# A chunked recurrence in 64x64 products: half of the heads keep their token rows in the other half of the partitions

## The reference

```python
def step(state, inp):
    r_t, w_t, k_t, v_t, a_t, b_t = inp
    sa = jnp.einsum('bhij,bhj->bhi', state, a_t)
    state = state * w_t[:, :, None, :] + sa[..., None] * b_t[:, :, None, :] + v_t[..., None] * k_t[:, :, None, :]
    return state, jnp.einsum('bhij,bhj->bhi', state, r_t)
...
mean = jnp.mean(y, axis=-1, keepdims=True)
var = jnp.mean(jnp.square(y - mean), axis=-1, keepdims=True)
yn = ((y - mean) * lax.rsqrt(var + GN_EPS)).reshape(B, S, RWKV_DIM) * gn_w + gn_b
bonus = (jnp.sum(r * k * r_k, axis=-1, keepdims=True) * v).reshape(B, S, RWKV_DIM)
return (yn + bonus) * g
```

## Time and profile before

| | before |
|---|---|
| median of 3 runs | 3677.74 us |
| profiled execution | 3676.37 us, span 3674.2 us |
| TensorE busy | 3536.7 us, 96% |
| VectorE busy | 1827.8 us, 50% |
| ScalarE busy | 1145.6 us, 31% |
| GpSimd busy | 490.6 us, 13% |

### The profile page before, as it was taken

One profiled execution on the slowest core, in us unless ns is written; L12 is line 12 of the kernel. 1 busy time (PEld: TensorE's weight loads), 2 busy tenths in 40 slices (PEclk: granted clock), 3 DMA queues, 4 the chain that ended last, 5 costly groups with the idle time before them and its releaser, 6 DMA issues. The chain is left out here.

```text
span 3674.2 us, 52665 instructions
## 1 busy us (share of the span) xinstructions
PE 3536.7 (96%) x21944; PEld 2888.8 (79%) x21944; DVE 1827.8 (50%) x2090; ACT 1145.6 (31%) x1325; POOL 490.6 (13%) x445
## 2 busy tenths in 40 slices
PE   7999999899999999999999999999999998999998
PEld 5578888778888888887578887887778996768886
DVE  7655244335244563346655244564786554455242
ACT  3632123222122232222632134233662222232222
POOL 1111011011011011010111013000241111111011
PEclk9999999889999999999999999999999998999998
DMA  3132323212322323223133323343321113313231
GB/s 124 60 96 92 102 93 97 69 58 94 101 92 92 103 92 103 92 95 107 60 96 95 100 92 104 103 132 95 95 73 60 38 44 130 103 46 103 92 103 58
DMA packets 313946, 329.07 MB, mean 90 GB/s; under 512 B 22819, under 2 KB 305446, under 8 KB 313255
## 3 DMA queue, kind: packets, MB, share of 16 engines
q1 hardware_dynamic: 306999, 302.87, 25.9%
q0 software_dynamic: 4464, 19.40, 1.6%
q10 hardware_dynamic: 2304, 4.20, 0.3%
HBM read 311.76 MB, written 14.68 MB: 89 GB/s over the span
## 5 line engine op out<-in xcount | busy, mean ns | idle before, releaser
L476 PE MATMUL ps<-xh,wh 128*128 128x512 f32 x2424 | 959.4, 396 | 24.4 <-DVE wl L417 21.0
L476 PE MATMUL ps<-xl,wh 128*128 128x512 f32 x2424 | 946.2, 390 | 0.0
L476 PE MATMUL ps<-xh,wl 128*128 128x512 f32 x2424 | 946.2, 390 | 0.0
L417 DVE TENSOR_TENSOR wl<-raw,wh 128x2048 fp32r<-128x2048 f32 (+2 forms) x287 | 642.6, 2240 | 457.4 <-ACT wh L412 456.8
L412 ACT ACTIVATE wh<-raw 128x2048 fp32r<-128x2048 f32 (+2 forms) x287 | 527.1, 1837 | 712.3 <-PE ps L476 678.2
L476 PEld LDWEIGHTS ps<-xh,wh 128*128 128x128 f32 x2424 | 457.0, 189 | 134.8 <-issue 36.2
L476 PEld LDWEIGHTS ps<-xl,wh 128*128 128x128 f32 x2424 | 457.2, 189 | 99.3 <-issue 5.8
L476 PEld LDWEIGHTS ps<-xh,wl 128*128 128x128 f32 x2424 | 456.8, 188 | 96.0
L476 PE MATMUL ps<-hh,wh 128*128 128x512 f32 x1280 | 498.3, 389 | 1.2 <-DVE wl L417 0.9
L476 PE MATMUL ps<-hl,wh 128*128 128x512 f32 x1280 | 497.9, 389 | 0.0
L476 PE MATMUL ps<-hh,wl 128*128 128x512 f32 x1280 | 497.9, 389 | 0.0
(11 more groups left out here) (403 smaller groups left out, 3660.4 us busy)
## 6 DMA issues: line engine op xcount, KB each, us to landing
raw<-in_mlp_w SPq DMA_DIRECT2D x128, 1024.0 KB, 5.2
raw<-in_ffn_w SPq DMA_DIRECT2D x32, 1024.0 KB, 5.3
raw<-in_w_in SPq DMA_DIRECT2D x31, 1024.0 KB, 5.3
raw<-in_a_w_in SPq DMA_DIRECT2D x20, 1024.0 KB, 5.0
raw<-in_c_w_in SPq DMA_DIRECT2D x12, 1024.0 KB, 5.1
raw<-in_a_w_out SPq DMA_DIRECT2D x16, 640.0 KB, 4.1
raw<-in_b_w_in SPq DMA_DIRECT2D x8, 1024.0 KB, 5.3
raw<-in_xa_wkv SPq DMA_DIRECT2D x8, 1024.0 KB, 5.6
```

The costliest lines, as they stand in the source:

```text
L417: nc.vector.tensor_tensor(wl[:, p.slot(su), 0:n], raw[:, p.slot(su), 0:n], wh[:, p.slot(su), 0:n], ALU.subtract).then_inc(lower, 1)
L476: last = nc.tensor.matmul(banks[mt][:, 0:st.n], wt[at_, slot, k, mt * P:mt * P + P], ops[oi][at_, kk, 0:st.n], start=k == 0 and su == 0 an ...
```

## The change

Heads of group 1 (q 4-7) keep everything that is indexed by token (TM, X, V, B and K turned, U, TLB, TLK) in the other half of the partitions: `toks(h, q)` is half h for q below 4 and the other half above, `chan(h, q)` is always h. Their products then have operands on one half and output on the other, or as before where both are channels or both tokens. `together` issues products in turn: for each i, both halves of the first list, then both halves of the second, which may be group 1 beside group 0, or two different steps.

The transposed inverse Z is summed in PSUM: `first_z` starts a bank of each group, `more_z` of each level accumulates onto it, and ScalarE copies the sum out after each level; VectorE's additions to Z go. X starts from a copy of a product too (`first_x`). The products and transposes of the next chunk move into the levels of this one as fillers; V and B are turned into one pair of banks and copied together. Where group 1 accumulates a product over operands on one half onto one over the other half, TensorE waits for itself (`ck_crossed`). The state's additions are done by VectorE after the X copies of the next chunk. The head norm's sums and spread alternate between both halves, and the scaling is done in two halves. Many semaphores elsewhere share a name now, with the counts adjusted; nothing else changes there.

```diff
+    def chan(h, q):
+        return HP[h]
+    def toks(h, q):
+        return HP[h] if q < 4 else HP[1 - h]
+    def together(*fns):
+        for i in range(4):
+            last = [[fn(h, i) for h in range(2)][-1] for fn in fns]
         return last
...
+            first_x = lambda h, q: mm(ps[YX[q // 4]][toks(h, q), cols(q)], TI[toks(h, q), q], i64[toks(h, q), :], start=True, stop=True)
+            first_z = lambda h, q: mm(ps[ZB[q // 4]][chan(h, q), cols(q)], i64[toks(h, q), :], TI[toks(h, q), q], start=q % 4 == 0, stop=True, skip_group_check=True)
+            more_x = lambda h, q: mm(ps[YX[q // 4]][toks(h, q), cols(q)], Z[chan(h, q), q], Yt[chan(h, q), q], start=True, stop=True)
+            more_z = lambda h, q: mm(ps[ZB[q // 4]][chan(h, q), cols(q)], Yt[chan(h, q), q], Z[chan(h, q), q],
+                                     start=False, stop=True, skip_group_check=True)
...
             for l in range(1, 6):
-                for g in range(2):
-                    pe.wait_ge(s(f"ck_x{g}"), 5 * c + l)
-                    heads_of(g, lambda h, q: mm(ps[YB[g]][h, cols(q)], TM[l % 2][h, q], X[h, q], start=True, stop=True)).then_inc(s(f"ck_y{g}"), 1)
...
+                times = lambda h, q: mm(ps[YX[q // 4]][chan(h, q), cols(q)], TM[l % 2][toks(h, q), q], X[toks(h, q), q],
+                                        start=True, stop=True)
+                pe.wait_ge(s("ck_x0"), 5 * c + l)
+                pe.wait_ge(s("ck_tm"), 6 * c + l + 1)
+                together(group(0, times))[0].then_inc(s("ck_y0"), 1)
+                if l > 1:
+                    pe.wait_ge(s("ck_y_copied1"), 5 * c + l - 1)
+                    pe.wait_ge(s("ck_z1"), 6 * c + l - 1)
+                    last = together(group(1, more_x), group(1, more_z))
...
+                if l == 4 and more:
+                    pe_products(pe, c + 1, 0, "ck_bprod")
...
+                pe.wait_ge(s("ck_y_copied0"), 5 * c + l)
+                pe.wait_ge(s("ck_z0"), 6 * c + l)
+                if l < 5:
+                    together(group(0, more_x))[0].then_inc(s("ck_xm0"), 1)
+                pe.wait_ge(s("ck_x1"), 5 * c + l)
+                last = together(group(0, more_z), group(1, times))
...
+            together(group(0, ds_b), group(1, ds_b))
+            together(group(0, ds_k), group(1, ds_k))[1].then_inc(s("ck_ds"), 1)
+            together(group(0, o_u), group(1, o_u))[1].then_inc(s("ck_crossed"), 1)
+            together(group(0, o_state))
+            pe.wait_ge(s("ck_crossed"), 2 * c + 2)
+            together(group(1, o_state))[0].then_inc(s("ck_yout"), 1)
...
+    def act_z(act, c, g, l):
+        act.wait_ge(s(f"ck_zm{g}"), 6 * c + l + 1)
+        act.activation(half(Z, g), half(b3(ZB[g]), g), ACT.Copy).then_inc(s(f"ck_z{g}"), 1)
```

More of the change, by code:

```diff
@@ L1602, in build @@
+        pool.wait_ge(s("pool_tables"), 4)
     mm = nc.tensor.matmul
     PB = (0, 1)
[L1605 to L1613, removed]
-        tok = slice(c * CH, c * CH + CH)
[L1616 to L1628, removed]
+    YX, ZB = (4, 5), (6, 2)
+    WB = (7, 3)
+    def chan(h, q):
[5 more added lines that the diff above has]
+            last = [[fn(h, i) for h in range(2)][-1] for fn in fns]
+        return last
@@ new lines, in group, with pe_turn, turn @@
+    def group(g, fn):
+        return lambda h, i: fn(h, 4 * g + i)
+    def pe_turn(pe, c, which, banks):
+        tok = slice(c * CH, c * CH + CH)
+        srcs_ = ((lambda h, q: VT[chan(h, q), q, tok], c64, 0), (lambda h, q: BT[chan(h, q), c, q], i64, 1)) if which == 0 \
+            else ((lambda h, q: KT[chan(h, q), c, q], i64, 0),)
+        def turn(src, eye, at_):
+            return lambda h, q: mm(ps[banks[q // 4]][toks(h, q), at_ * 256 + q % 4 * CH:at_ * 256 + q % 4 * CH + CH],
+                                   src(h, q), eye[chan(h, q), :], start=True, stop=True)
+        for e in srcs_:
+            last = together(group(0, turn(*e)), group(1, turn(*e)))
+        last[-1].then_inc(s("ck_turned"), 1)
@@ L1630, in HB, with pe_products, product, SB @@
+    def pe_products(pe, c, which, done):
+        def product(h, q):
+            k = chan(h, q)
+            return mm(ps[PB[q // 4]][toks(h, q), q % 4 * P:q % 4 * P + P], (BT, KT)[which][k, c, q],
+                      AR[k, c, q].rearrange("p a n -> p (a n)"), start=True, stop=True)
+        together(group(0, product), group(1, product))[-1].then_inc(s(done), 1)
+    RT = small[:, 4:12]
     def HB(c):
-        return 3 if c < NC - 1 else 4
+        return 0 if c < NC - 1 else 6
+    def SB(c):
+        return (0, 1) if c < NC - 1 else (4, 5)
@@ L1633, in pe_head_sums @@
     def pe_head_sums(pe, c):
         pe.wait_ge(s("hd_squared"), c + 1)
[L1636 to L1637 removed]
+        for i in range(4):
+            for g in range(2):
+                last = mm(ps[HB(c)][HP[g], 2 * i:2 * i + 2], hs[c][:, 4 * g + i], headones[:, 0:P:64], start=True, stop=True)
         last.then_inc(s("hd_sums"), 1)
@@ L1642, in pe_head_spread @@
         pe.wait_ge(s("hd_inverse"), c + 1)
[L1643 to L1646, removed]
+        for i in range(4):
+            for g in range(2):
+                for e in range(2):
+                    last = mm(ps[SB(c)[g]][HP[e], cols(4 * g + i)], RT[HP[g], 2 * i + e:2 * i + e + 1].to_broadcast([64, CH]),
+                              i64[HP[g], :], start=True, stop=True)
         last.then_inc(s("hd_spread"), 1)
@@ L1686, in pe_chunks @@
                     if c:
+                        if more:
+                            pe.wait_ge(s("ck_turned_copied"), 4 * c + 6)
+                        pe_head_sums(pe, c - 1)
                         pe.wait_ge(s("ck_state"), c)
[L1688 to L1695, removed]
@@ L1736, in pe_chunks @@
-            last.then_inc(s("ck_yout"), 1)
-            if c < NC - 1:
-                pe_turns(pe, c + 1)
+                    pe.wait_ge(s("ck_kmasked"), c + 1)
+                    together(group(0, w0_tok), group(1, w0_tok))[1].then_inc(s("ck_crossed"), 1)
+                if l == 3:
+                    together(group(0, w0_state))[0].then_inc(s("ck_w0"), 1)
+                    pe.wait_ge(s("ck_crossed"), 2 * c + 1)
+                    together(group(1, w0_state))[0].then_inc(s("ck_w0"), 1)
+                    if c:
+                        pe_head_spread(pe, c - 1)
@@ new lines, in pe_chunks @@
+            pe.wait_ge(s("ck_z0"), 6 * c + 6)
+            together(group(0, u_of))[0].then_inc(s("ck_u"), 1)
+            if more:
+                pe.wait_ge(s("ck_bmasked"), c + 2)
+                pe_products(pe, c + 1, 1, "ck_kprod")
+            pe.wait_ge(s("ck_z1"), 6 * c + 6)
+            together(group(1, u_of))[0].then_inc(s("ck_u"), 1)
+            last = together(group(0, o_v), group(1, o_v))
+            if more:
+                pe.wait_ge(s("ck_turned_copied"), 4 * c + 8)
+            pe.wait_ge(s("ck_u_copied"), 2 * c + 2)
@@ L1767, in act_chunks @@
                 if l == 2 and c:
                     act_head_root(act, c - 1)
+                if l == 3:
+                    for g in range(2):
+                        act.wait_ge(s("ck_w0"), 2 * c + g + 1)
+                        act.activation(half(W0, g), half(b3(WB[g]), g), ACT.Copy).then_inc(s("ck_w0_copied"), 1)
+                if l == 5 and more:
+                    act_turned_k(act, c + 1)
+                act_y(act, c, 1, l)
+                act_z(act, c, 0, l)
+            act_z(act, c, 1, 5)
```

317 lines of the change are left out of this document (166 added, 151 removed).

## The result

Before, 3677.74 us (median); after, 3657.39 us (3655.83 to 3661.78, five runs). The ratio is 0.9947, its 95% interval 0.9935 to 0.9959. Forecast were 3617 us and a range of 3594 to 3660. The profiled execution of after has a span of 3655.9 us.

The account below looks back on a forecast made before the run. TensorE, filled with many small matmuls, was taken as the recurrence's bound. Terms -7.0 - 6 x 7.8 - 5 - 3.0 = -62, +1 for fetch, took 3676.37 us to 3617 (chance 0.64); own range 3597 to 3642, overall 3594 to 3660.

Parts of the forecast that it names:

- Four corners at 35 ns a product: Recurrence: 304 four-cornered products an inner chunk fall from 58.4 to 35 ns each, -7.1 us a chunk.
- the bound of 29.2 ns a product: Recurrence: fastest pace allowed for four-cornered products, four streams each with a record per 58.4 ns; worth -14 us on the forecast.
- drain: Rival, chance 0.06: changing between straight and crossed corners drains TensorE's array, 168 changes a chunk, 15 us; about 3795 us.
- issue floor: Rival, chance 0.16: over long four-cornered runs records leave TensorE's queue more slowly, 24 ns each; 3648 us.
- Head spread of the last chunk, 1.97 us to 1.0: Last chunk's final spread now uses both row halves: 1.97 us at the lower clock becomes 1.0.
- The start, 8.3 us to 5.3: Recurrence's start, from TensorE's first product to L1676: 8.3 us becomes 5.3, so -3.0 us.
- Waits, 2.4 us an inner chunk, longest at L1700 for Yt after level 5: TensorE's waits in an inner chunk: 2.4 us against 1.7 before, +0.7; longest for ScalarE's Yt copy after level 5.
- I put +1 for instruction fetch: Allowance of +1 us in the whole sum for TensorE's program being read in pieces, turning -62 into -61.
- The rival "instruction fetch": Chance 0.06: each of the recurrence's 60 program pieces costs 0.3 us, +18 us, 3635 us.
- The sign "a chunk's waits exceed 5 us": Stated sign of a wrong prediction: TensorE's waits above 5 us a chunk; then look at ScalarE's order of copies.
- The range 3594 to 3660: Range for the whole kernel's time, stated to hold both the forecast (3617 us) and the issue floor (3648 us).
- streaming columns, not of issue: TensorE's bursts: a product of N=128 costs 112.5 ns, twice N=64, so column streaming sets the time.

Follow-up runs that it names:

- the added work: Against the changed kernel, the squaring products stream 128 columns instead of 64 in three of four cases, same instructions: 3662.40 us.
- the bursts alone: A program of TensorE's matmul bursts only, the whole computation left out; four corners with 64 columns took 28 ns a record over ten pieces, 62.54 to 98.45 us.
- the 39 spare loads: Changed kernel plus 19 or 20 spare products of 16 columns, read by nobody, at the end of chunks 1 to 6: 3674.62 us.
- long packets: Changed kernel with the two spilled arrays stored by chunk, so slice loads use 2 KB packets instead of 256 bytes: 3657.54 us, ratio 0.9939.
- fewer instructions: Changed kernel with 112 TensorE instructions fewer a chunk: wide products start the inverse and make the head norm's sums and spread; 3650.64 us.
- 48 instructions fewer: Changed kernel with the inverse started by 4 products of 256 columns a chunk instead of 16 of 64: 3658.43 us.

## Why the prediction was wrong, step by step

- *Four corners at 35 ns a product*: right, and too careful. 14.7 to 15.2 ns a record is about the bound of 29.2 ns a product. No drain, and no issue floor: no run shows one of 24 or 25 ns a record. TensorE's busy time fell by 63 us, the size of the whole forecast.
- *Head spread of the last chunk, 1.97 us to 1.0*: 0.69 us.
- *The start, 8.3 us to 5.3*: the first product at 2790.22, L1697 at 2795.53, 5.31 us: right.
- *Waits, 2.4 us an inner chunk, longest at L1700 for Yt after level 5*: right. Counted as the 1.7 us of before were, from start to start of TensorE's loads less one step, the waits for other engines are 2.3 to 2.6 us an inner chunk (the view lists only idle times over 0.15 us), and L1700's for ScalarE's Yt, 4.6 us in 8, lead them. VectorE 13.4 us a chunk (forecast near 14), ScalarE 12.3 (some 14).
- *"I put +1 for instruction fetch"*: this is the step that failed. I had counted 60 pieces and divided them into the time, one per 4.1 us and then per 3.1, without asking how fast pieces can come. They cost 37.4 us more of issue waits than before (38.8 less 1.4). Take these off the 240.7 us and 203.3 remain, against the forecast 200.4; the granted clock, 0.98 instead of 0.99, is some 2.4 of the rest, an estimate (1% of 240.7).
- *The rival "instruction fetch"* had the mechanism and the wrong price: 0.3 us a piece, read off a slow chunk of before, where two corners take 256 x 14.6 ns = 3.7 us a piece, longer than a fetch. Its 18 us should have been: 304 products a chunk are 1216 instructions, 4.75 pieces; each needs 3.5 us and would run, at 35 ns a product, in 2.2; 4.75 x 1.3 x 7.8 = 48 us, some of it made up in two-cornered stretches. That gives at most 3664, an estimate in hindsight. The four issue waits of before already end 2.4 to 2.8 us behind a piece's start; they would have told.
- *The sign "a chunk's waits exceed 5 us"* came true (6.5 to 12.6 us an inner chunk, counted in the same way, issue waits included), but the place to look at that it named, ScalarE's order of copies, had no part in it.
- *The range 3594 to 3660* holds the 3657.39 us by luck: it reached that far for the issue floor (3648), which isn't what happened; the forecast's own mechanism ended at 3642.

## What to carry to other kernels

When a change makes instructions faster, put beside the engine's new time the rate at which its program comes: in unrolled code here 256 instructions per 3.5 us, 13.7 ns each. Where the new time is below that, fewer and wider instructions are what helped here, and added columns are partly free: 128 columns took 29 ns a record where 64 took 28 in the bursts alone, and half of the added work was free in the kernel. Look at when the pieces start, not only at how many there are; and do not count on moving their ends about.

## What the hardware showed

- Four 64x64 corners at once: 14.7 ns a float32 record within a piece, 28 over ten pieces.
- A product of 16 columns costs a corner what one of 64 does: the spare records start 58 ns apart on each corner, as those of 64 columns. From 64 to 128 columns the two-cornered record goes from 29.2 ns to 56.3; the prediction's "streaming columns, not of issue" rests on these two and doesn't hold below 64.
- A straight list starts when six records of the crossed list before it are still to start, without being issued in turn (all eight such changes in one trace): on different corners the starts leave the program's order.
- The granted clock fell to 0.50 for 3.4 us after TensorE had stood for 2.7 us, having run at 1.00 until then, so a stop for program was paid for a second time. What exactly brings it down these runs do not tell: in after it fell behind two of the four stops over 1.75 us (3.1 and 2.6 us long) and not behind the others (1.9 and 2.6). With the 39 spare loads it also fell twice within a chunk (at 2940.90 and 2975.03), behind stops of 1.3 and 1.6 us.
- Open: whether long packets bring anything (ratios 0.9939 against 0.9947 alone, 0.9914 against 0.9926 with fewer instructions; the intervals overlap in both pairs), why 48 instructions fewer brought nothing, and how a piece's fetch is queued among other transfers.
